# One TensorE transpose group, three VectorE operations and one subtraction moved in a hybrid encoder block

## What is computed

```python
ha = rms_norm(ha, mlstm_norm_g[l]).reshape(B, S, D_MLSTM).astype(dt)
y_a = ha * jax.nn.sigmoid(o_a) * jax.nn.silu(z_a)
...
g = jax.nn.sigmoid(gate.astype(jnp.float32)).astype(dt).reshape(B, S, N_BRANCH, D_MODEL)
merged = (g[:, :, 0] * (y_a @ w_branch[l, 0])
          + g[:, :, 1] * (y_b @ w_branch[l, 1])
          + g[:, :, 2] * (y_m @ w_branch[l, 2]))
x = x + merged @ w_out[l]
```

## Time and profile before

| what | value |
| --- | --- |
| median of 3 runs | 957.99 us (957.79 to 958.44) |
| profiled execution | 957.99 us |
| its span | 956.2 us |
| PE busy | 950.4 us, 99% of the span |
| DVE busy | 733.0 us, 77% |
| ACT busy | 544.8 us, 57% |
| POOL busy | 349.0 us, 37% |

### The profile page before, as it was taken

One profiled execution on the slowest core, in us unless ns is written; L12 is line 12 of the kernel. 1 busy time (PEld: TensorE's weight loads), 2 busy tenths in 40 slices (PEclk: granted clock), 3 DMA queues, 4 the chain that ended last, 5 costly groups with the idle time before them and its releaser, 6 DMA issues. The chain is left out here.

```text
span 956.2 us, 13763 instructions
## 1 busy us (share of the span) xinstructions
PE 950.4 (99%) x5041; PEld 843.6 (88%) x5041; DVE 733.0 (77%) x1110; ACT 544.8 (57%) x834; POOL 349.0 (37%) x246
## 2 busy tenths in 40 slices
PE   9999999999999999999999999999999999999998
PEld 7888888888989988988988888898998989998877
DVE  6879987688996686685688566896776957984896
ACT  6877644465456546546563422595765857874341
POOL 0200834456327137146120071362613527102910
PEclk9999999999999999999999999999999999999999
DMA  8624222144531631532354335716043150538412
GB/s 293 236 88 132 87 91 71 61 133 133 165 94 61 173 106 53 150 110 72 113 194 172 126 108 157 231 32 200 1 123 109 33 154 1 177 129 306 182 45 88
DMA packets 105158, 119.31 MB, mean 125 GB/s; under 512 B 4772, under 2 KB 80136, under 8 KB 104332
## 3 DMA queue, kind: packets, MB, share of 16 engines
q1 hardware_dynamic: 105084, 118.53, 38.4%
q10 hardware_dynamic: 16, 0.00, 0.0%
HBM read 106.45 MB, written 12.07 MB: 124 GB/s over the span
## 5 line engine op out<-in xcount | busy, mean ns | idle before, releaser
L825 PE MATMUL proj<-hT_hi,w_hi 128*128 128x512 f32 x264 | 104.0, 394 | 0.0
L825 PE MATMUL proj<-hT_hi,w_lo 128*128 128x512 f32 x264 | 103.1, 390 | 0.0
L825 PE MATMUL proj<-hT_lo,w_hi 128*128 128x512 f32 x264 | 102.9, 390 | 0.0
L2233 DVE TENSOR_TENSOR w_lo<-w_raw,w_hi 128x2048 fp32r<-128x2048 f32 x25 | 61.6, 2465 | 44.2 <-ACT w_hi L1480 41.3
L1480 ACT ACTIVATE w_hi<-w_raw 128x2048 fp32r<-128x2048 f32 x24 | 45.9, 1914 | 57.4 <-PE proj L825 55.8
L825 PE MATMUL proj<-y_hi,w_hi 128*128 128x512 f32 x192 | 75.2, 391 | 0.0
L825 PE MATMUL proj<-y_hi,w_lo 128*128 128x512 f32 x192 | 74.8, 390 | 0.0
L825 PE MATMUL proj<-y_lo,w_hi 128*128 128x512 f32 x192 | 74.7, 389 | 0.0
L825 PEld LDWEIGHTS proj<-hT_hi,w_lo 128*128 128x128 f32 x264 | 49.6, 188 | 10.5
L825 PEld LDWEIGHTS proj<-hT_lo,w_hi 128*128 128x128 f32 x264 | 49.6, 188 | 9.9
L825 PEld LDWEIGHTS proj<-hT_hi,w_hi 128*128 128x128 f32 x264 | 49.6, 188 | 9.8
(11 more groups left out here) (591 smaller groups left out, 3141.2 us busy)
## 6 DMA issues: line engine op xcount, KB each, us to landing
w_raw<-w_in_in SPq DMA_DIRECT2D x36, 512.0 KB, 4.6
w_raw<-w_in_in SPq DMA_DIRECT2D x56, 256.0 KB, 3.6
w_raw<-w_branch_in SPq DMA_DIRECT2D x12, 1024.0 KB, 5.5
merged<-w_in_in SPq DMA_DIRECT2D x38, 256.0 KB, 3.7
merged<-w_in_in SPq DMA_DIRECT2D x18, 512.0 KB, 5.8
w_raw<-w_mem_kv_in SPq DMA_DIRECT2D x10, 512.0 KB, 6.1
yF<-x_in SPq DMA_DIRECT2D x8, 512.0 KB, 9.9
w_raw<-w_in_in SPq DMA_DIRECT2D x4, 1024.0 KB, 5.3
```

The source lines that it names most:

```text
L825: ins = mm(ps, lhs[a](k, k0), rhs[b](k, k0), start=(first and k == 0 and j == 0), stop=(last and k == KH - 1 and j == 2))
L2233: V.tensor_tensor(w_lo[:, kh, :, 0:n], w_raw[:, kh, :, 0:n], w_hi[:, kh, :, 0:n].bitcast(F32), ALU.subtract).then_inc(w_lo_done, 1)
```

## The change

It has three edits.

1. PE: `a_turn_h(g)` is issued ahead of gate product 5, no longer behind it.
2. DVE: `gate_sum(1, 1)` goes ahead of `gate_add(4)`, and `gate_add(5)` goes behind `gate_sum(1, 2)` and `gate_low(8)`.
3. The subtraction that makes `out_s3` leaves DVE's list and stands in POOL's, behind `out_sum(4)`, with the same two waits.

```diff
@@ PE
             gate_product(4, h_half_sum(3), second_pair, False, lambda f: (u_saved, G_SAVED + f + 3))
+            a_turn_h(g)
             gate_product(5, h_half_sum(0), first_pair, False, lambda f: (u_saved, G_SAVED + f + 5))
-            a_turn_h(g)
             gate_product(6, h_half(KH, HALF_T), first_pair, False, lambda f: (u_added, G_ADDED + f + 5))
@@ DVE
             gate_low(7)
+            gate_sum(1, 1)
             gate_add(4, mid, g_block(0, 1, 0), 6)
-            gate_sum(1, 1)
-            gate_add(5, low, g_block(0, 1, 1), 4)
             gate_sum(1, 2)
             gate_low(8)
+            gate_add(5, low, g_block(0, 1, 1), 4)
             gate_sum(1, 3)
@@ DVE
             dve.wait_ge(g_merged, 12)
             out_low_part(1)
-            dve.wait_ge(op_low, A_OPLOW + OUT_OPS + 1)
-            V.tensor_tensor(out_s3, merged_k[:, 0:KH, 0:HALF_T], merged_k[:, 0:KH, HALF_T:S], ALU.subtract).then_inc(s_made, 1)
             split_lo(GA[0] + 1, 1, 512)
@@ POOL
             out_sum(4, out_b21, out_b21, out_b22)
             first_half, second_half = merged_k[:, 0:KH, 0:HALF_T], merged_k[:, 0:KH, HALF_T:S]
+            pool.wait_ge(op_low, A_OPLOW + OUT_OPS + 1)
+            pool.wait_ge(g_merged, 12)
+            G.tensor_tensor(out_s3, first_half, second_half, ALU.subtract).then_inc(s_made, 1)
             pool.wait_ge(s_made, A_SMADE + 2)
```

## The result

The changed kernel takes 965.62 us (median of 6 runs, 962.64 to 967.19), the kernel before 958.14 us (6 runs, 957.77 to 958.51). The ratio is 1.0075 with a 95% interval of 1.0060 to 1.0089: slower by 7.5 us, inside the range of 960.6 to 966.0, but 2.7 us above the forecast of 962.9. The runs of the change also lie farther apart, 4.6 us against 0.7.

The account below looks back on a forecast made before the run. PE was taken as the bound, busy 950.4 of 956.2 us. To 957.99 us the forecast added 2.05 for the gate products and 2.9 for out_s3 on POOL, giving 962.9 us, range 960.6 to 966.0.

Parts of the forecast that it names:

- The sum for the two waits: Whole kernel: PE's delays of 2.05 us at the gates and 2.9 us before output product 1 add, giving 962.9 us.
- rival R3: PE before output product 1: 3.7 us idle drops the clock to 1.2 GHz, 2.8 us more, 965.7 us; chance 0.12.
- the bounds of the two waits alone: Whole kernel: with both parts' bounds, the time lies from 961.6 to 964.0 us.
- PE bound, each late operand costs in full: Whole kernel: PE busy 950.4 of 956.2 us; an edit making its next operand late costs its whole lateness.
- Part 1: Gate products: product 6 waits for the later gate_add(5), +2.38 us, 0.33 given back at product 9: +2.05 us.
- The walk over DVE's list: DVE at the gates: gate_add(5) begins at 848.62, so PE starts product 6 at 849.18 instead of 846.80.
- Part 2: Output end: out_s3 on POOL ends at 912.35 instead of 899.32, delaying ACT, DVE and PE's output product 1: +2.9 us.
- The rule of turns: DVE and POOL at the output end: their shared port pair is locked for a whole instruction, so they alternate.
- R1: POOL at the output end: out_s3 done by 907, PE's 0.81 us pause goes, 959.2 us; chance 0.07.
- R2: Output end: POOL's chain doesn't move with PE, so the gate delay hides in the later wait, 960.9 us; chance 0.10.
- SP's issue behind product 11: DMA issued at 864.93 feeds POOL's first subtraction, so POOL's chain moves with PE and both delays add.

Follow-up runs that it names:

- fillers: Whole change plus useless matmuls on PE, 12 before output product 1 and 14 between gate products 5 and 6: 963.06 us, ratio 1.0051 against the kernel before.
- the two gate runs: Against the kernel before: PE's and DVE's gate edits without the out_s3 move, 960.82 us; DVE's gate order alone, 960.67 us.
- the run with the pause filled: Kernel before with only out_s3 moved to POOL, plus 12 useless matmuls on PE before output product 1: 961.13 us, ratio 1.0029.
- `out_s3` sooner: Kernel before with only out_s3 moved to POOL, but ahead of out_sum(4) instead of behind it: 959.15 us, ratio 1.0005.
- the kernel with a wait of 3.84 us alone: Kernel before with only out_s3 moved to POOL behind out_sum(4), no useless matmuls: 963.18 us, ratio 1.0053.

## Why the prediction came out as it did

The sum for the two waits was right. The rest of the 7.5 us, some 2.7, is the clock, for which the sum had no term. That the median still lies inside the range is owed to the place that rival R3 had been given in it: the bounds of the two waits alone ended at 964.0.

- **PE bound, each late operand costs in full.** Right. With the clock held up by fillers the two parts cost 4.8 us, and their waits stand in the list.
- **Part 1, +2.05 us.** Right in size: 0.23 + 2.01 - 0.33 = 1.9 in the trace, +2.4 and +2.3 in the medians of the two gate runs, which hold some falls of the clock, +2.2 and +2.0 in their runs at 1.00. The walk over DVE's list was right to 0.01 us: with the 0.54 us added, `gate_add(5)` begins at 848.62 and PE's product 6 at 849.18, both as forecast. The late start of the transposes is no cost of its own: without that edit product 6 waits for the same add.
- **Part 2, +2.9 us.** Right: 3.96 - 1.04 = 2.92 in the trace, 2.9 in the run with the pause filled. The walk had POOL's last subtraction 1.2 us after DVE's low part ended (1.15 in the trace), L3028 first, then `out_s3` 2.35 us (2.26), ACT, and DVE's idle time. The rule of turns holds in the rows shown here. For `out_s3` sooner it came out 0.6 us short in the chain (L3039 over at 912.98, expected 912.4) and 0.45 us in the time (959.15, expected 958.7).
- **R1, POOL keeps up.** False: `out_s3` ended at 913.85, where R1 needed 907. Nor did the one sooner place that was tried make it come true: with the end of `out_s3` at 905 the third edit alone still takes 959.15, since POOL's other work then collides with DVE.
- **R2, one delay hides the other.** False: by R2 the whole change would cost 2.9 us without the clock, and it costs 4.8; alone the parts cost 2.0 to 2.4 and 2.9. SP's issue behind product 11 moved from 864.93 to 866.36, with the 0.54 us by 1.97, and POOL's first subtraction from 878.50 to 880.12.
- **R3, the clock falls.** This is what the sum left out. It had a chance of 0.12, for which no row was named, and it happened in eight of nine runs. The forecast had said itself that the clock's digits can't speak for a pause of 3.7 us, and then held the clock at its top all the same. At the gates it wasn't thought of at all, though the forecast had PE idle there for 2.1 us, and there it falls in part of the runs. Its price was not right either: 2.8 us for half of product 1's matmuls, while in the trace eight of 24 were slow and cost 1.54 us. That R3's 965.7 us is so close to the measured 965.62 is luck: a single fall gives some 964, and the median is made of several. The forecast value of 962.9 us is what a run takes without a fall, 962.64; the median lies 3 us above it.

What stays open: the runs at 0.995 lost 4.2 us against the one at 1.00, nearly three times the 1.5 us of the profiled fall, with only two pauses. With the third edit alone, which has one long pause, three of five runs were 1.5 us longer than the other two, so that pause can cost twice; with one fall at the gates that would make three. The mean clocks fit. As an estimate, the traced stretch at 0.50, from 925.7 to 929.1, takes 0.0018 from the mean over the span; two such stretches take 0.0035 and three 0.0053, and these are the 0.998, 0.996 and 0.995 of the table. No such run was traced, so this is argued and not shown.

## What to carry to other kernels

Before moving an operation off a busy engine, look at what that engine does with the time: here DVE only waited longer for ACT, while the operation's new place stood behind four subtractions on POOL that nobody needed yet. When two engines hand work to each other in turns, walk both lists after a move, since a step moved for one engine's sake can stall the other either way. And a new pause of some microseconds on PE is to be priced with the clock that may fall after it: here one pause of 3 us more cost 1.9 us on top, and a new pause of 2 us let the clock fall in some runs at one place, for 1.6 us, and in no run at another.

## What was not expected of the hardware

- The granted clock fell to 0.50 after a step of 2.14 us without matmuls. It was under 1.00 in two of six runs each of the kernels that had the gate pause alone, and in all five of the kernel with a wait of 3.84 us alone, but in none of eleven with a step of 2.15 us before output product 1. In the three falls that were traced it fell 0.8, 1.2 and 1.3 us after PE had taken up its work again, not in the pause. The kernel before, with steps up to 1.04 us at these places, was at 1.00 in all of its runs.
- Matmuls without a use, put into a pause, made a kernel faster: 961.13 against 963.18 us with the same edit and 12 matmuls more (from separate groups).
